# Rows of 272 values instead of 264 in two activation tiles of a two-block transformer kernel

## The chip, the cores and the metric

The kernel is one program on one core of a Trainium2 chip. The metric is the device time of one execution in microseconds (us). All arithmetic is float32; the large products are made from float32r operands, in which each factor is split into a high and a low part.

## The reference

256 tokens of width 1024 go through two blocks of two layers each. The first block is conditioned by vectors c and c_ctx: each layer has shifts, scales and gates from `silu(c) @ ada_w`. Its layers are a latent attention over 256 context and 256 own tokens, and a gated MLP with a token mixing; each is followed by a feed-forward layer of 4096:

```python
h = rmsnorm(x, g) * (1 + scale) + shift
x = x + g_m * mixer(h)
x = x + g_f * (square(relu(modulate(x) @ w1)) @ w2)
```

The second block has an even layer (gated linear attention in chunks of 64, and attention in a sliding window) and an odd layer (attention in blocks), each with one wide input projection of a normed x and one output projection. All matrices of weights are read from HBM once: some 190 MB.

## The kernel before, in words

The program writes out one stream of instructions for each engine and orders them with semaphores. Activations lie transposed: 128 features on the partitions, 256 tokens along the row, so a tensor of width 1024 is 8 k tiles of one row each.

The matrices come in chunks of 128 x 1024 values (512 KB) through a ring of 4 slots (`raw`). For each chunk ScalarE copies the float32r high part into `w_hi` (L1147), and VectorE writes `raw - w_hi` into `w_lo` (L1577). TensorE then makes every product of a weight tile and an activation row three times (`split_product`): L527 high by high, L528 weights' high part by the activation's low part, L529 weights' low part by the activation's high part. Each of the three is a weight load of 128 x 128 and a matmul that streams the row. Eight k tiles of three products make one group, whose sum stands in a PSUM bank; VectorE or ScalarE reads it out, and the other of two (or four) banks is filled meanwhile.

The activation rows are read from these tiles:

- `act_hi`, `act_lo`: 8 rows each, 264 values long (ACT_W). 256 are tokens; in the first block two more columns (256 and 257) hold the shift, so that one product makes both, and streams 258 columns (`act_and_shift`). Stages ffn0_up (32 groups), gm_u0 (8) and ffn1_up (32) read 258 columns; even_s, even_a, even_g, odd_g, odd_k and odd_q (37 groups) read 256 (`act`). Two token projections, even_av and odd_v, and the scores of the latent attention use parts of the rows as the weights.
- `hid_hi`, `hid_lo`: 32 rows of 256, read in ffn0_down and ffn1_down (32 groups of 24 products each).
- `s_hi`, `s_lo`: 16 rows of 256, read in gm_v (as weights), gm_u1 and gm_out; `om`, `oe`, `oo`: 8 rows of 256, read by the output projections of the attentions.

ffn0_down follows ffn0_up directly, and ffn1_down follows ffn1_up. In the up stages VectorE also scales each group (L1636), ScalarE applies relu and splits (L1380, L1383), GpSimd squares and subtracts (L2182, L2186), and VectorE takes the products for the next layers' shifts and scales (L1592), whose weights stream through a ring of their own. SyncE issues the loads in the order of use.

Two small tensors concern the change as well. `gqk` (128 x 1) is the product of two gains, written by VectorE at L1728, and the scale of the keys' eviction on ScalarE (L1289) and VectorE (L1760). `rms_gla` (8 x 128) holds the roots of the linear attention's mean squares: ScalarE writes it (L1167, called in L1513), VectorE inverts it (L2059), and TensorE spreads it over the partitions (L1063). `rstd` (128 x 512) holds the reciprocal roots of the token norms; behind the latent attention only columns 0 to 257 are in use.

SBUF is laid out in the order of the declarations, and tensors of different layers share addresses. In the even layer it is full to the last 128 bytes of a partition. By that order, `act_hi`, `act_lo`, `hid_hi`, `hid_lo`, `s_hi`, `s_lo`, `om` and `oo` begin at 64 bytes past a multiple of 256 in each partition, `w_hi`, `w_lo` and `oe` at 128.

Of the kernel before, what the change touches and what calls it, by code (L numbers as in the profile page):

```python
# [22 lines left out]
P = 128  # L23
D = 1024
KT = D // P
S = 256
CTX = 256
SC = S + CTX
H = 8
Q_LORA, KV_LORA, ROPE = 384, 256, 64  # L30
# [3 lines left out]
RING = 4  # L34
ADA_FIRST = 16
QK = 192
ACT_W = S + 8
TAU = 16.0
EPS = 1e-6
NEG = -1e30  # L40
# [106 lines left out]
def build_program(nc, vecs, consts, gm_rows, c_rows, rel_ext, x_in, ctx_in, ada, weights,  # L147
                  gm_ws, gla_w_up, out):
    fp32, fp32r = mybir.dt.float32, mybir.dt.float32r
    ALU, ACT, AX = mybir.AluOpType, mybir.ActivationFunctionType, mybir.AxisListType  # L150
# [10 lines left out]
    with hold:  # L161
        def sb(name, shape, dt=fp32, stack=hold):
            return stack.enter_context(nc.sbuf_tensor(name, shape, dt))

        def sem(name):
            return hold.enter_context(nc.semaphore(name))
# [12 lines left out]
        mod_in = sb("mod_in", [P, 2 * KT, 2])  # L179
        mods = sb("mods", [P, ADA_MODS, KT])  # L180
        gain = sb("gain", [P, 5, KT])
        eps_q = sb("eps_q", [P, 2])
        act_hi = sb("act_hi", [P, KT, ACT_W], fp32r)
        act_lo = sb("act_lo", [P, KT, ACT_W], fp32r)
        scaled = sb("scaled", [P, 2, S + 2])
# [4 lines left out]
        rstd = sb("rstd", [P, SC])  # L190
# [8 lines left out]
        with ExitStack() as mla:  # L199
            with ExitStack() as first:  # L200
                in_f32 = sb("mla_in", [P, 2, SC], fp32, first)
                in_hi = sb("mla_in_hi", [P, 2, SC], fp32r, first)
                in_lo = sb("mla_in_lo", [P, 2, SC], fp32r, first)
                ada_more = sb("ada_more", [P, 4, CW], fp32, first)
                unused = sb("products", [P, CW], fp32, first)
            kn_hi = sb("kn_hi", [P, H, SC], fp32r, mla)
            v_mla = sb("v_mla", [P, 4, H * P], fp32, mla)
            with ExitStack() as first:
                ctx = sb("ctx", [P, KT, CTX], fp32, first)
                sq_ctx = sb("sq_ctx", [P, KT, CTX], fp32, first)  # L210
                ckv = sb("ckv", [P, 2, SC], fp32, first)
                sq_lora = sb("sq_lora", [P, 3, SC], fp32, first)
                silu_ctx = sb("silu_ctx", [P, CW], fp32, first)
            kn_lo = sb("kn_lo", [P, H, SC], fp32r, mla)
            qr_hi = sb("qr_hi", [P, H // 2, S], fp32r, mla)
            qr_lo = sb("qr_lo", [P, H // 2, S], fp32r, mla)
            kpe_hi = sb("kpe_hi", [P, SC], fp32r, mla)
            kpe_lo = sb("kpe_lo", [P, SC], fp32r, mla)
            k_rstd_hi = sb("k_rstd_hi", [H, SC], fp32r, mla)
            k_rstd_lo = sb("k_rstd_lo", [H, SC], fp32r, mla)  # L220
            om_hi = sb("om_hi", [P, KT, S], fp32r, mla)
            om_lo = sb("om_lo", [P, KT, S], fp32r, mla)
            p_mla = sb("p_mla", [P, 2, SC], fp32, mla)
            pt_mla = sb("pt_mla", [P, 2, 4, S], fp32, mla)
            heads = sb("heads", [H, H], fp32r, mla)
            q_scale = sb("q_scale", [P, 2, 2, H], fp32, mla)
            gqk = sb("gqk", [P, 1], fp32, mla)
        late = hold.enter_context(ExitStack())
        bias = sb("bias", [P, 16, S], fp32, late)
        anti = sb("anti", [P, P], fp32, late)  # L230
# [16 lines left out]
        with ExitStack() as even:  # L247
            masks = sb("masks", [P, 2 * S + P], fp32, even)
            aq = sb("aq", [P, 2, S], fp32, even)
            ak = sb("ak", [P, 2, S], fp32, even)  # L250
            z_state = sb("z_state", [P, 4, S], fp32, even)
            z, zl = z_state[:, 0:2, :], z_state[:, 2:4, :]
            state = z_state[:, 0:3, :].rearrange("p n (t d) -> p n t d", t=2)
            cum = sb("cum", [P, 2, S], fp32, even)
            e_pos = sb("e_pos", [P, 2, S], fp32, even)
            e_neg = sb("e_neg", [P, 2, S], fp32, even)
            e_last = sb("e_last", [P, 2, S], fp32, even)
            down, w_up = e_last[0:16, 0, :], e_last[0:16, 1, :]
            qe = sb("qe", [P, 2, S], fp32, even)
            ke = sb("ke", [P, 2, S], fp32, even)  # L260
            kl = sb("kl", [P, 2, S], fp32, even)
            decay = sb("decay", [P, 2, 2, 4], fp32, even)
            kl_tok = sb("kl_tok", [P, 2, 2, P], fp32, even)
            av = sb("av", [P, 2, 512], fp32, even)
            att = sb("att", [P, H, P], fp32, even)
            bq = sb("bq", [P, 4, S], fp32, even)
            bk = sb("bk", [P, S], fp32, even)
            bv = sb("bv", [P, S], fp32, even)
            bv_tok = sb("bv_tok", [P, 2, P], fp32, even)
            gate = sb("gate", [P, H, S], fp32, even)  # L270
            rms_gla = sb("rms_gla", [H, P], fp32, even)
            o_gla = e_last
            logit = sb("logit", [P, 2, S], fp32, even)
            late_held = sb("late_held", [P, 2, S], fp32, even)
            held = [scaled[:, 0, 0:S], scaled[:, 1, 0:S], late_held[:, 0, :], late_held[:, 1, :]]
            prob = sb("prob", [P, 2, S], fp32, even)
            prob_t = sb("prob_t", [P, 4, 2, P], fp32, even)
            oe_hi = sb("oe_hi", [P, KT, S], fp32r, even)
            oe_lo = sb("oe_lo", [P, KT, S], fp32r, even)
# [12 lines left out]
        bank = [hold.enter_context(nc.psum_tensor(f"bank{i}", [P, 512], fp32)) for i in range(8)]  # L292
# [72 lines left out]
        cq_high, q_eps = sem("cq_high"), sem("q_eps")  # L365
# [1195 lines left out]
        def _(dve):  # L1561
# [18 lines left out]
            def modulate(a):  # L1580

                m, o = divmod(a, KT)
                dve.wait_ge(ada_in[a % RING], 16 * (a // RING + 1))
                dve.tensor_tensor_reduce(ada_raw[:, a % RING, :], ada_raw[:, a % RING, :], silu_row[:], 1.0,
                                         V("ada_b0", 2 * KT + a, 1), ALU.mult, ALU.add,
                                         mods[:, m, o:o + 1]).then_inc(ada_used, 1)
# [135 lines left out]
            modulate(1)  # L1722
            convert(11)
            dve.wait_ge(lora_sums, 1)
            dve.tensor_scalar(eps_q[:], bank[7][:, 0:2], EPS / Q_LORA, EPS * EPS, ALU.mult, ALU.add).then_inc(q_eps, 1)
            modulate(2)
            convert(12)
            dve.tensor_tensor(gqk[:], V("q_g_nope"), V("k_g_nope"), ALU.mult).then_inc(gqk_ready, 1)  # L1728
# [639 lines left out]
```

## Time and profile before

| | |
|---|---|
| median of 3 runs | 980.67 us (978.28 to 981.75) |
| the profiled execution | 979.0 us |
| its span, first to last instruction | 977.2 us |
| mean granted clock of TensorE | 0.977 |
| TensorE busy | 933.1 us, 95% |
| VectorE busy | 704.9 us, 72% |
| ScalarE busy | 537.5 us, 55% |
| GpSimd busy | 308.9 us, 32% |
| DMA | 195.60 MB, 200 GB/s |

The profile is of one execution, so its numbers are compared with 979.0 us. PE is the matmul side of TensorE, PEld its weight loads, which run beside the matmuls. A matmul's duration reaches over the start of the next ones, because they are pipelined: how fast they follow each other is read from their starts, or from how many there are in a window.

### The profile page before, as it was taken

Reading aid. Unit: us, or ns where it says so; the run is one execution under the profiler, and the core shown is the slowest. Engines: PE = TensorE matmul, PEld = TensorE weight load, DVE = VectorE, ACT = ScalarE, POOL = GpSimd, SP = SyncE. Lnnn points to the kernel's source line nnn. Section 1 sums busy time; section 2 is a strip of 40 time slices with the busy share of each in tenths; the row PEclk is TensorE's granted clock in tenths of the full one; section 3 lists DMA queues with packets and bytes.
Section 4 is the critical chain, followed back from the end, with each engine's and each line's share of the span. In section 5 each row is a group of like instructions: output and inputs, shape, how many; then the busy total and the mean of one; then the engine's idle time right before and its main releaser. Section 6 shows DMA issues by size and latency. Waiting matters only on the chain.

```text
span 977.2 us, 19548 instructions
## 1 busy us (share of the span) xinstructions
PE 933.1 (95%) x6882; PEld 861.5 (88%) x6882; DVE 704.9 (72%) x1132; ACT 537.5 (55%) x921; POOL 308.9 (32%) x272
## 2 busy tenths in 40 slices
PE   5988989999999999999979999999999999999996
PEld 5877556799999999988969999999999879899996
DVE  3997678678889788897886698555555873575764
ACT  3565655565666444655634666655444771674644
POOL 1952022227898011120051288640110000330012
PEclk9898999999999999999979999999999998999999
DMA  9856175167877988788615676555565332255421
GB/s 348 291 190 225 41 232 178 43 237 262 321 278 266 309 287 293 246 321 285 231 66 174 235 257 217 185 182 192 187 199 174 122 108 87 87 173 185 160 88 43
DMA packets 57052, 195.60 MB, mean 200 GB/s; under 512 B 6303, under 2 KB 9791, under 8 KB 56736
## 3 DMA queue, kind: packets, MB, share of 16 engines
q1 hardware_dynamic: 55312, 192.36, 58.0%
q0 software_dynamic: 1680, 2.44, 1.1%
q8 instruction: 37, 0.61, 0.3%
q14 instruction: 23, 0.19, 0.1%
HBM read 192.65 MB, written 1.07 MB: 198 GB/s over the span
## 4 chain that ended last, share of the span: by engine, by line
PE 84%; DVE 9%; ACT 3%; issue 3%; DMA 1%; POOL 0%; SPq 0%; DVEq 0%; ACTq 0%
PE bank L527 24%; PE bank L529 23%; PE bank L528 23%; DVE w_lo L1577 2%; PE bank L792 1%; PE bank L926 1%; PE bank L952 1%; PE bank L625 1%; ACT w_hi L1147 1%; PE bank L783 1%; DMA x<-x_in 1%; PE bank L825 1%; PE bank L634 1%; DVE ada_raw L1679 1%; PE bank L880 1%
## 5 line engine op out<-in xcount | busy, mean ns | idle before, releaser
L1577 DVE TENSOR_TENSOR w_lo<-raw,w_hi 128x1024 fp32r<-128x1024 f32 (+1 forms) x261 | 338.7, 1300 | 101.9 <-ACT w_hi L1147 99.4
L1147 ACT ACTIVATE w_hi<-raw 128x1024 fp32r<-128x1024 f32 (+1 forms) x261 | 272.4, 1045 | 166.6 <-PE bank L529 156.0
L527 PE MATMUL bank<-act_hi,w_hi 128*128 128x258 f32 (+1 forms) x872 | 251.1, 288 | 0.0
L529 PE MATMUL bank<-act_hi,w_lo 128*128 128x258 f32 (+1 forms) x872 | 247.5, 284 | 0.0
L528 PE MATMUL bank<-act_lo,w_hi 128*128 128x258 f32 (+1 forms) x872 | 246.1, 282 | 0.0
L527 PEld LDWEIGHTS bank<-act_hi,w_hi 128*128 128x128 f32 x872 | 166.5, 191 | 3.3 <-issue 2.8
L528 PEld LDWEIGHTS bank<-act_lo,w_hi 128*128 128x128 f32 x872 | 166.7, 191 | 1.0 <-issue 1.0
L529 PEld LDWEIGHTS bank<-act_hi,w_lo 128*128 128x128 f32 x872 | 165.6, 190 | 0.0
L528 PE MATMUL bank<-hid_lo,w_hi 128*128 128x256 f32 x512 | 141.4, 276 | 0.0
L527 PE MATMUL bank<-hid_hi,w_hi 128*128 128x256 f32 x512 | 141.4, 276 | 0.0
L529 PE MATMUL bank<-hid_hi,w_lo 128*128 128x256 f32 x512 | 141.4, 276 | 0.0
L528 PEld LDWEIGHTS bank<-hid_lo,w_hi 128*128 128x128 f32 x512 | 96.1, 188 | 0.0
L527 PEld LDWEIGHTS bank<-hid_hi,w_hi 128*128 128x128 f32 x512 | 96.1, 188 | 0.0
L529 PEld LDWEIGHTS bank<-hid_hi,w_lo 128*128 128x128 f32 x512 | 96.1, 188 | 0.0
L2182 POOL TENSOR_TENSOR tile_f<-relu 128x256 f32<-128x256 f32 x64 | 80.4, 1257 | 30.9 <-ACT relu L1380 30.9
L2186 POOL TENSOR_TENSOR hid_lo<-tile_f,hid_hi 128x256 f32 x64 | 75.1, 1173 | 18.0 <-POOL tile_f L2182 18.0
L2134 POOL TENSOR_TENSOR square_sum<-square_sum,sq 128x256 f32<-128x256 f32 x30 | 38.7, 1290 | 131.7 <-ACT sq L1179 131.7
L1592 DVE CUSTOM_DVE_ANT_0 ada_raw<-ada_raw,silu_row 128x1024 f32<-128x1024 f32 x56 | 75.8, 1354 | 2.3 <-DMA ada_raw<-ada 2.0
L2126 POOL TENSOR_TENSOR s_lo<-tile_f,s_hi 128x256 fp32r<-128x256 f32 x24 | 23.4, 993 | 98.2 <-ACT s_hi L1152 98.2
L527 PE MATMUL bank<-s_hi,w_hi 128*128 128x256 f32 x192 | 54.1, 282 | 0.0
L528 PE MATMUL bank<-s_lo,w_hi 128*128 128x256 f32 x192 | 53.7, 279 | 0.0
L529 PE MATMUL bank<-s_hi,w_lo 128*128 128x256 f32 x192 | 53.7, 279 | 0.0
(349 smaller groups left out, 1815.0 us busy)
## 6 DMA issues: line engine op xcount, KB each, us to landing
raw<-weights SPq DMA_DIRECT2D x247, 512.0 KB, 4.0
ada_raw<-ada SPq DMA_DIRECT2D x88, 512.0 KB, 4.9
raw<-weights SPq DMA_DIRECT2D x14, 384.0 KB, 4.6
ada_more<-ada SPq DMA_DIRECT2D x8, 512.0 KB, 6.6
bias<-bias_by_distance SPq DMA_DIRECT2D x1, 2048.0 KB, 9.3
x<-x_in SPq DMA_DIRECT2D x1, 1024.0 KB, 7.7
ctx<-ctx_in SPq DMA_DIRECT2D x1, 1024.0 KB, 9.7
out<-result SPq DMA_DIRECT2D x4, 256.0 KB, 2.7
```

Of the source, the lines that this page charges most:

```text
L527: pe.matmul(dst, w[0], a[0], start=start, stop=False)
L528: pe.matmul(dst, w[0], a[1], start=False, stop=False)
L529: return pe.matmul(dst, w[1], a[0], start=False, stop=stop)
L625: last = pe.matmul(bank[at_bank][:, 0:S], mean[:], source[:, k, :], start=k == 0, stop=k == KT - 1)
L634: last = pe.matmul(bank[6 + k % 2][:, 0:2], first_ada(2 * k)[:, j * P:(j + 1) * P], silu_c[:, j, :], start=j == 0, stop=j == KT - 1)
L1147: act.activation(w_hi[:, slot, 0:width_of(c)], raw[:, slot, 0:width_of(c)], ACT.Copy).then_inc(weight_hi, 1)
L1577: dve.tensor_tensor(w_lo[:, slot, 0:w], raw[:, slot, 0:w], w_hi[:, slot, 0:w].bitcast(fp32), ALU.subtract).then_inc(weight_lo, 1)
L1592: dve.tensor_tensor_reduce(ada_raw[:, q, :], ada_raw[:, q, :], silu_row[:], 1.0, 0.0, ALU.mult, ALU.add, ada_col[:, q:q + 1]).then_inc(ada ...
L2126: pool.tensor_tensor(lo, tile_f32[:, i % 4, :], hi.bitcast(fp32), ALU.subtract).then_inc(split_lo, 1)
L2134: pool.tensor_tensor(square_sum[:], sq[:, 0, :] if k == 1 else square_sum[:], sq[:, k, :], ALU.add).then_inc(square_sums, 1)
L2182: pool.tensor_tensor(tile_f32[:, i % 4, :], relu[:, g % 2, :], relu[:, g % 2, :], ALU.mult).then_inc(hid_squared, 1)
L2186: pool.tensor_tensor(hid_lo[:, ds(it * 8 + g, 1), :], tile_f32[:, i % 4:i % 4 + 1, :], hid_hi[:, ds(it * 8 + g, 1), :].bitcast(fp32), ALU. ...
```

## The change

ACT_W goes from S + 8 = 264 to S + 16 = 272 values, so a row of `act_hi` and `act_lo` takes 1088 bytes instead of 1056, and each tile 8704 instead of 8448. What is read and written of a row is as before. `gqk` becomes the third column of `eps_q`, and `rms_gla` a part of `rstd`: 8 partitions, columns 384 to 511.

```diff
-ACT_W = S + 8
+ACT_W = S + 16
...
-        eps_q = sb("eps_q", [P, 2])
+        eps_q = sb("eps_q", [P, 3])
...
-            gqk = sb("gqk", [P, 1], fp32, mla)
+            gqk = eps_q[:, 2:3]
...
-            rms_gla = sb("rms_gla", [H, P], fp32, even)
+            rms_gla = rstd[0:H, SC - P:SC]
...
-            dve.tensor_scalar(eps_q[:], bank[7][:, 0:2], EPS / Q_LORA, EPS * EPS, ALU.mult, ALU.add).then_inc(q_eps, 1)
+            dve.tensor_scalar(eps_q[:, 0:2], bank[7][:, 0:2], EPS / Q_LORA, EPS * EPS, ALU.mult, ALU.add).then_inc(q_eps, 1)
```

S is 256, SC 512, P 128 and H 8.

## Rows read from the trace of the kernel before

**Rows 1.** The page, part 1: busy us, share of the span, instructions.

```profile
PE 933.1 (95%) x6882; PEld 861.5 (88%) x6882; DVE 704.9 (72%) x1132; ACT 537.5 (55%) x921; POOL 308.9 (32%) x272
```

**Rows 2.** The page, part 4: the chain that ended last, by engine and line.

```profile
PE 84%; DVE 9%; ACT 3%; issue 3%; DMA 1%; POOL 0%; SPq 0%; DVEq 0%; ACTq 0%
PE bank L527 24%; PE bank L529 23%; PE bank L528 23%; DVE w_lo L1577 2%; PE bank L792 1%; PE bank L926 1%; PE bank L952 1%; PE bank L625 1%; ACT w_hi L1147 1%; PE bank L783 1%; DMA x<-x_in 1%; PE bank L825 1%; PE bank L634 1%; DVE ada_raw L1679 1%; PE bank L880 1%
```

**Rows 3.** Windows: from:to us, length, busy by engine (instructions), PE clock, DMA, GB/s.

```profile
230.00:300.00 70.00, 70.00 (x587) 70.00 (x586) 59.90 (x76) 44.98 (x73) 59.49 (x47) 1.00 0.85 299
310.00:390.00 80.00, 80.00 (x708) 80.00 (x708) 65.47 (x80) 37.23 (x47) 14.27 (x11) 1.00 0.86 291
470.00:486.00 16.00, 16.00 (x144) 16.00 (x143) 15.72 (x30) 10.62 (x17) 0.00 (x0) 1.00 0.61 209
510.00:550.00 40.00, 40.00 (x342) 40.00 (x341) 24.50 (x28) 19.37 (x27) 7.68 (x6) 1.00 0.53 171
854.00:866.00 12.00, 12.00 (x102) 12.00 (x102) 11.11 (x19) 9.62 (x17) 6.33 (x5) 1.00 0.72 226
876.00:896.00 20.00, 20.00 (x172) 20.00 (x171) 10.06 (x13) 9.51 (x14) 0.00 (x0) 1.00 0.47 150
575.00:640.00 65.00, 65.00 (x545) 65.00 (x545) 46.33 (x58) 42.48 (x68) 51.28 (x47) 1.00 0.65 211
655.00:730.00 75.00, 75.00 (x664) 75.00 (x663) 42.80 (x42) 33.67 (x42) 8.83 (x6) 1.00 0.60 190
```

**Rows 4.** Groups by line and shape, whole span: count, busy us, mean ns of one.

```profile
L527 PE MATMUL bank<-act_hi,w_hi 128*128 128x258 f32 x576 | 163.8, 284 | 0.0
L528 PE MATMUL bank<-act_lo,w_hi 128*128 128x258 f32 x576 | 161.9, 281 | 0.0
L528 PE MATMUL bank<-hid_lo,w_hi 128*128 128x256 f32 x512 | 141.4, 276 | 0.0
L528 PE MATMUL bank<-act_lo,w_hi 128*128 128x256 f32 x296 | 84.2, 284 | 0.0
```

**Rows 5.** Timeline, 304.1 to 307.0 us, L527 alone: start us, duration us.

```profile
304.11 0.29 PE L527 MATMUL bank<-act_hi,w_hi 128*128 128x258 f32 x1
...
304.48 0.29 PE L527 MATMUL bank<-act_hi,w_hi 128*128 128x258 f32 x1
...
304.84 0.28 PE L527 MATMUL bank<-act_hi,w_hi 128*128 128x258 f32 x1
...
305.20 0.28 PE L527 MATMUL bank<-act_hi,w_hi 128*128 128x258 f32 x1
...
305.56 0.28 PE L527 MATMUL bank<-act_hi,w_hi 128*128 128x258 f32 x1
...
305.92 0.28 PE L527 MATMUL bank<-act_hi,w_hi 128*128 128x258 f32 x1
...
306.28 0.28 PE L527 MATMUL bank<-act_hi,w_hi 128*128 128x258 f32 x1
...
306.63 0.28 PE L527 MATMUL bank<-act_hi,w_hi 128*128 128x258 f32 x1
...
306.99 0.29 PE L527 MATMUL bank<-hid_hi,w_hi 128*128 128x256 f32 x1
```

**Rows 6.** The tiles gqk and rms_gla: durations ns (min/median/max), first and last start.

```profile
L1728 DVE TENSOR_TENSOR gqk<-vec x1: 155/155/155, 74.9 to 74.9; 128x1 f32<-128x1 f32 x1
L1289 ACT ACTIVATE kn_hi<-bank,gqk x8: 681/682/683, 101.1 to 117.7; 128x512 fp32r<-128x512 f32 x8
L1760 DVE SCALAR_TENSOR_TENSOR kn_lo<-bank,gqk,kn_hi x8: 750/751/752, 101.9 to 118.4; 128x512 fp32r<-128x512 f32 x8
L1063 PE MATMUL bank<-rms_gla,const x16: 270/270/371, 842.3 to 844.1; 8*128 8x128 f32 x16
L2059 DVE RECIPROCAL rms_gla<-rms_gla x1: 940/940/940, 841.3 to 841.3; 8x128 f32<-8x128 f32 x1
```

## The prediction

> **What bounds the kernel now.** I read the engines' shares first: TensorE is busy 95% of the span, the weight loads that run beside it 88%, VectorE 72%, the others less [rows 1]. The chain that ended last says the same by another road: 84% of it lies on PE, and the three lines of the split product (L527, L528, L529) hold 70% of it [rows 2]. So the time is a count of fp32r products times the distance from one start to the next, wherever the products run gaplessly. The windows inside the dense stages give that distance: the window's length plus the 0.28 us that one product lasts, over the count of PE. In each of these windows PE is busy from end to end and its clock is the full 2.4 GHz. An edge can miscount one product, which is 0.2% in the long windows and 1% in the 12 us one.
>
> The answer is not one number [rows 3]:
> - rows of `act`, 258 columns (ffn0_up, ffn1_up): 70.28/587 = 119.7 ns and 65.28/545 = 119.8 ns
> - rows of `act`, 256 columns (odd_g): 20.28/172 = 117.9 ns
> - rows of `hid`, 256 columns (ffn0_down, ffn1_down): 80.28/708 = 113.4 ns and 75.28/664 = 113.4 ns
> - rows of `s`, 256 columns: 16.28/144 = 113.1 ns in gm_u1, but 40.28/342 = 117.8 ns in gm_out
> - rows of `oe`, 256 columns (even_out): 12.28/102 = 120.4 ns
>
> The mean durations of one product say the same: 276 ns from `hid`, 281 to 284 from `act` [rows 4]. The clock and the number of columns do not explain this: `hid`, `s` and `oe` have the same width, and two columns are 0.8 ns at 2.4 GHz. What differs is where a row begins. A row of `hid` or `s` is 1024 bytes, so all begin at one place modulo 256 (64, by the order and the sizes of the tensors). `oe` begins at 128 modulo 256, and the weights too. `act` rows are 1056 bytes apart, which is 4 x 256 + 32, so the eight k tiles step through 64, 96, 128, ... 32. But `s` shows that place is not all: the same rows cost 113.1 in one stage and 117.8 in another. There is some locking between the stream of moving rows and the stream of weight loads, into which a stage falls when it starts.
>
> **The change, part by part.**
>
> *gqk into a third column of eps_q.* It is written once (155 ns) and read as a scale by 8 ScalarE and 8 VectorE instructions [rows 6]. The instructions, their order and their waits stay; eps_q stays within the 32 bytes that it occupied. I take 0. The trace has no pair that differs in this alone; a bound either way is the whole write, 0.16 us.
>
> *rms_gla into rstd, partitions 0 to 7, columns 384 to 511.* The same root, reciprocal (940 ns) and 8 products (16 records of 270 ns) as before, in the same order [rows 6]. The row scaling of this layer reads columns 0 to 257 of rstd, so no new hazard and no wait. I take 0. Where both bounds matter, the largest thing in it is the reciprocal on the path, and 10% of that is 0.1 us each way. These two edits free 32 and 512 bytes, which is room for the longer rows (2 tiles x 8 rows x 32 bytes = 512). Everything behind the two tiles moves by 512 bytes or by nothing, so the place modulo 256 of all other operands stays.
>
> *Rows of 272.* No instruction is added, removed or widened: the products still read 258 or 256 columns. Rows are now 1088 bytes apart, 4 x 256 + 64. k tiles 0 to 7 begin at 64, 128, 192, 0, 64, 128, 192, 0, so all eight at multiples of 64, where now only the four even ones do. act_lo begins 256 bytes later, the same place modulo 256. What can change is the distance of 576 x 3 = 1728 products of 258 columns [rows 4] and of 296 x 3 = 888 of 256 columns. 144 more have an `act` row as the weights (16 of scores, 16 of each token projection on each of three lines); at 1% of the about 0.12 to 0.23 us that one lasts they hold 0.3 us either way, and I take 0.
>
> No row shows rows that are 64 apart modulo 256. The nearest ones:
> (a) The even rows of today's tiles already begin at multiples of 64. In the last group of ffn0_up, the starts of L527 are 0.37, 0.36, 0.36, 0.36, 0.36, 0.36, 0.35, 0.36 us apart for k = 0 to 7 [rows 5]. Even rows: 0.37 + 0.36 + 0.36 + 0.35 = 1.44; odd rows: 4 x 0.36 = 1.44. The aligned half is no cheaper. If all eight become like the even ones, the change is 0, with 0.02 us in 2.88 as reading error, 0.7% of 1728 x 0.12 = 207 us: 1.4 us either way.
> (b) The upper spacing of 64-aligned rows, 117.8 in gm_out, plus 0.8 for two columns: 1728 x (119.7 - 118.6) = 1.9 us gained, 888 x (117.9 - 117.8) = 0.1: together 2.0.
> (c) The lower spacing, 113.4 and 114.2: 1728 x 5.5 = 9.5 and 888 x 4.5 = 4.0, together 13.5 us gained. This is the lower end.
> (d) That of `oe`: taken at its round value of 120.0 within its 1%, 1728 x 1.1 + 888 x 2.1 = 3.8 us lost. This is the upper end for these products.
>
> I take the middle of (a) and (b), 1.0 us gained: (a) is measured on the very rows, the width and the weights concerned, and (b) and (c) come from tiles whose place stays fixed from k to k, which this change doesn't bring: the place still moves at each k, just in other steps. So I expect no lock on the fast spacing.
>
> The Trainium skill, page "TensorE: Matmul & The Clock Gate", section "Step-by-step: what each phase is for", says that streaming and weight loading have read ports of their own, so that loading doesn't take bandwidth from the running product; "SBUF — State Buffer", section "SBUF: two separate sides", puts a cost only on crossing 16-byte lines, and 1056 and 1088 are both multiples of 16. By these the change is worth exactly nothing. The spread of 113.1 to 120.4 ns at one width and clock disagrees with the first, so I don't let it decide.
>
> *What covers and what comes late.* If `act` products speed up, VectorE and GpSimd must keep up: in 230 to 300 us they are busy 59.90 and 59.49 of 70 us [rows 3], so 2.46 and 2.44 us of a group's 24 x 119.7 = 2.87. Even the fast case leaves 2.74. ScalarE has less, and 299 GB/s would have to become 313 in (c), which the trace doesn't show; if DMA stays at 299, ffn0_up (32 of the 72 groups) keeps its 9.5 x 32/72 = 4.2 us.
>
> **Sum.** The profiled execution took 979.0 us (span 977.2 and 1.8 around it). 979.0 - 1.0 = 978.0; its median of three runs is 980.67, 1.7 above, so 979.7. This kernel's runs differ by 0.3%, 2.9 us, so less than that counts as the same.
>
> **Rivals.**
> 1. *Fast lock.* Aligned rows let the `act` stages fall into the fast spacing wholly or in part. For it: both `hid` stages and gm_u1 have it, and all are 64-aligned. Against it: [rows 5] even rows gain nothing today. In full 13.5 us, 967.2; half of it (one width, or DMA holding ffn0_up) 974.
> 2. *The fast lock of ffn_down is lost (slower side).* ffn0_down and ffn1_down follow an `act` stage without a gap (the last start of [rows 5] is the first product of `hid`), and `s` shows that one tile can be in either state by how it is entered. If the new pattern of k hands over in another phase, 512 x 3 = 1536 products go from 113.4 to 117.8: 6.8 us. With the 1.0 gained: 980.67 + 5.8 = 986.5. It decides at the first product of ffn0_down, and holds for the stage. Against it: today both entries come out fast.
> 3. *Slow lock.* The `act` stages settle as `oe` does, case (d): 980.67 + 3.8 = 984.5.
> 4. *Nothing depends on the row's place*, as the ports' rule has it: 980.7.
>
> **Chances.** Forecast 0.37, fast lock 0.34, ffn_down lost 0.15, slow lock 0.08, nothing at all 0.06. Faster: 0.34. Same: 0.43 (forecast and 4). Slower: 0.23. The range reaches from 968, just inside the full fast lock, to 987, just over rival 2; I leave out some 0.08 below and 0.06 above. The forecast's own range is (b) to the upper reading error of (a): 978.7 to 982.1.
>
> **What would show it.** In windows of the same stages: 230 to 300 should count about 590 products (119 ns), 310 to 390 still 708, gm_out 342. A count of 612 or more in the first is rival 1, about 680 in 310 to 390 rival 2, 582 or fewer in the first rival 3. The L527 starts of one group should stay at 0.35 to 0.37 us, now repeating after four k instead of eight. PE counts, waits and the tail of the linear attention stay as they are; a longer stretch around 841 us would prove the two moved tiles wrong. The prediction is wrong if the distance in any dense stage moves by more than 1%.

## The result, and the profile after

The changed kernel takes 988.12 us in the median of 9 runs (982.62 to 990.08), the kernel before 980.92 (978.28 to 984.92, 9 runs). The ratio is 1.0055, 95% interval [1.0033, 1.0076]: slower, by some 5 to 7 us (the quotient of the two medians is 1.0073, inside the interval). The profiled execution took 988.59 us with a span of 986.6, so 9.4 us more span than before. In the runs below, one execution each of after_extra64 (1828.03 us), rows320 (1316.69 us) and the kernel before (1530.78 us) was slow as a whole; the medians hold them and the ratios don't.

The page of the changed kernel, part 1 and the first lines of part 4, against [rows 1, 2]:

```profile
PE 942.5 (96%) x6882; PEld 871.1 (88%) x6882; DVE 704.2 (71%) x1132; ACT 538.1 (55%) x921; POOL 308.8 (31%) x272
PE 82%; DVE 11%; issue 3%; ACT 3%; DMA 1%; POOL 0%; SPq 0%; DVEq 0%; ACTq 0%
PE bank L527 24%; PE bank L528 23%; PE bank L529 23%; DVE w_lo L1577 2%; PE bank L792 1%; DVE products L1679 1%; PE bank L926 1%; PE bank L625 1%; PE bank L952 1%; ACT w_hi L1147 1%; DVE ada_raw L1679 1%; PE bank L783 1%; DMA x<-x_in 1%; PE bank L825 1%; DVE ada_more L1679 1%
```

There are as many instructions as before. PE is busy 942.5 - 933.1 = 9.4 us longer, all of the difference; the others are as they were. The groups of part 5 say which products, against [rows 4]:

```profile
L528 PE MATMUL bank<-act_lo,w_hi 128*128 128x258 f32 (+1 forms) x872 | 246.4, 283 | 0.0
L528 PE MATMUL bank<-hid_lo,w_hi 128*128 128x256 f32 x512 | 143.9, 281 | 0.0
```

The `act` rows, the only ones whose step changed, are as slow as ever. The `hid` rows, which the change only moved by 512 bytes, went from 276 to 281 ns. The windows of the dense stages, columns as in [rows 3]:

```profile
230.00:300.00 70.00, 70.00 (x587) 70.00 (x586) 60.12 (x76) 45.17 (x73) 59.72 (x47) 1.00 0.86 301
310.00:390.00 80.00, 80.00 (x681) 80.00 (x680) 62.58 (x76) 36.21 (x46) 13.39 (x11) 1.00 0.82 283
470.00:486.00 16.00, 16.00 (x144) 16.00 (x143) 15.12 (x29) 10.21 (x16) 0.00 (x0) 1.00 0.65 214
575.00:640.00 65.00, 65.00 (x545) 65.00 (x544) 47.59 (x60) 42.30 (x69) 51.58 (x47) 1.00 0.66 217
655.00:730.00 75.00, 75.00 (x639) 75.00 (x639) 40.28 (x39) 31.97 (x39) 7.43 (x6) 1.00 0.58 188
```

In the `act` windows the counts are those of before, 587 and 545. In the two `hid` windows they are 681 for 708 and 639 for 664: 80.28/681 = 117.9 ns from product to product instead of 113.4. The `act` rows of 256 columns (odd_g) are as before too. The changed kernel has one product less than the kernel before [rows 3] in 20 us, which is within the edge error:

```profile
882.00:902.00 20.00, 20.00 (x171) 20.00 (x170) 10.38 (x15) 10.12 (x15) 0.00 (x0) 1.00 0.40 131
```

Whole stages, the changed kernel and then the kernel before:

```profile
217.90:307.00 89.10, 89.10 (x745) 89.09 (x745) 77.27 (x96) 58.18 (x92) 74.49 (x58) 1.00 0.83 288
307.10:397.40 90.30, 90.30 (x769) 90.30 (x768) 71.75 (x89) 40.54 (x51) 16.77 (x13) 1.00 0.81 281
651.10:741.40 90.30, 90.30 (x769) 90.30 (x769) 48.04 (x47) 39.71 (x48) 11.65 (x10) 1.00 0.57 186
851.00:875.50 24.50, 24.50 (x193) 24.50 (x193) 17.58 (x29) 15.78 (x30) 11.09 (x11) 0.93 0.46 147
881.50:922.30 40.80, 38.89 (x313) 38.47 (x312) 20.69 (x26) 19.18 (x26) 0.00 (x0) 0.96 0.48 157
```

```profile
217.80:306.90 89.10, 89.10 (x745) 89.10 (x745) 77.03 (x96) 58.20 (x92) 74.28 (x58) 1.00 0.81 287
307.00:393.90 86.90, 86.90 (x769) 86.90 (x768) 71.61 (x89) 40.17 (x51) 17.00 (x13) 1.00 0.86 293
647.70:734.70 87.00, 87.00 (x770) 87.00 (x769) 48.66 (x47) 39.34 (x48) 11.72 (x10) 1.00 0.61 192
844.30:867.40 23.10, 23.10 (x193) 23.03 (x193) 17.56 (x29) 15.79 (x30) 11.06 (x11) 1.00 0.50 158
873.40:912.80 39.40, 37.49 (x313) 37.07 (x312) 20.74 (x26) 19.21 (x26) 0.00 (x0) 1.00 0.51 167
```

ffn0_up takes 89.10 us in both. ffn0_down and ffn1_down take 3.4 and 3.3 us more: 6.7 of the 9.4. Another 1.4 + 1.4 us lie in even_out and odd_g, where the granted clock was 0.93 and 0.96 instead of 1.00 in this execution: for part of these stages it stood at the lower level (0.50 in 852 to 854 us). Is that the change or the execution? The other executions tell. Through the spans and mean clocks of 115 executions of the kernel before (from all rounds of the study) goes a straight line that falls by 8.3 us for each 0.01 of clock. The mean clock differs from run to run in both kernels alike: it is 0.970 to 0.979 in the nine executions of the changed kernel, 0.974 on average, and 0.973 on average in those 115. The two profiled executions differ by 0.004 (0.973 and 0.977), so about 3.3 us of the 9.4 go with the clock and not with the change. At equal clock the nine spans of the changed kernel lie 6.3 us above that line on average (4.9 to 8.7), which fits the 6.7 us of the two ffn_down stages. What is left is below 1 us in several places, of both signs; one of them is mla_out, where PE makes 108 products in 200 to 212 us instead of 104. The two moved small tensors cost nothing, as these lines of the changed kernel show beside [rows 6]:

```profile
L1289 ACT ACTIVATE kn_hi<-bank,eps_q x8: 680/682/684, 102.1 to 118.7; 128x512 fp32r<-128x512 f32 x8
L1063 PE MATMUL bank<-rstd,const x16: 270/270/371, 849.0 to 850.8; 8*128 8x128 f32 x16
```

### The profile page after: what moved, and what is told of

Same layout as the page of the kernel before. It is cut to its first block, busy times and chain, and to the rows that moved or that the text cites. A ratio compares the mean times of both kernels' runs of the same rounds, so it can differ in the third digit from the quotient of the medians.

```text
span 986.6 us, 19548 instructions
## 1 busy us (share of the span) xinstructions
PE 942.5 (96%) x6882; PEld 871.1 (88%) x6882; DVE 704.2 (71%) x1132; ACT 538.1 (55%) x921; POOL 308.8 (31%) x272
## 3 DMA queue, kind: packets, MB, share of 16 engines
q0 software_dynamic: 1680, 2.44, 1.1%
## 4 chain that ended last, share of the span: by engine, by line
PE 82%; DVE 11%; issue 3%; ACT 3%; DMA 1%; POOL 0%; SPq 0%; DVEq 0%; ACTq 0%
PE bank L527 24%; PE bank L528 23%; PE bank L529 23%; DVE w_lo L1577 2%; PE bank L792 1%; DVE products L1679 1%; PE bank L926 1%; PE bank L625 1%; PE bank L952 1%; ACT w_hi L1147 1%; DVE ada_raw L1679 1%; PE bank L783 1%; DMA x<-x_in 1%; PE bank L825 1%; DVE ada_more L1679 1%
## 5 line engine op out<-in xcount | busy, mean ns | idle before, releaser
L527 PE MATMUL bank<-act_hi,w_hi 128*128 128x258 f32 (+1 forms) x872 | 249.6, 286 | 0.0
L527 PEld LDWEIGHTS bank<-act_hi,w_hi 128*128 128x128 f32 x872 | 165.6, 190 | 3.3 <-issue 2.8
L527 PE MATMUL bank<-hid_hi,w_hi 128*128 128x256 f32 x512 | 143.9, 281 | 0.0
L528 PE MATMUL bank<-hid_lo,w_hi 128*128 128x256 f32 x512 | 143.9, 281 | 0.0
L529 PE MATMUL bank<-hid_hi,w_lo 128*128 128x256 f32 x512 | 143.9, 281 | 0.0
L527 PEld LDWEIGHTS bank<-hid_hi,w_hi 128*128 128x128 f32 x512 | 97.2, 190 | 0.0
L527 PE MATMUL bank<-s_hi,w_hi 128*128 128x256 f32 x192 | 54.1, 282 | 0.0
```

The source lines that it names most:

```text
L527: pe.matmul(dst, w[0], a[0], start=start, stop=False)
L528: pe.matmul(dst, w[0], a[1], start=False, stop=False)
L529: return pe.matmul(dst, w[1], a[0], start=False, stop=stop)
```

## The experiments

Each kernel ran beside the kernel before. In the table, the three counts are of PE in 230 to 300, 310 to 390 and 655 to 730 us (ffn0_up, ffn0_down, ffn1_down); 708 and 664 are the fast spacing, 681 and 639 the slow one. The counts are of one profiled execution each. rows320_width256 leaves out the two shift columns, so its output lacks the shifts.

| kernel | median us | ratio to before [95%] | ffn0_up | ffn0_down | ffn1_down |
|---|---|---|---|---|---|
| before | | | 587 | 708 | 664 |
| changed | 988.12 | 1.0055 [1.0033, 1.0076] | 587 | 681 | 639 |
| rows264_rest512 | 980.82 | 1.0011 [0.9987, 1.0035] | 587 | 709 | 664 |
| edits_only | 981.49 | 1.0005 [0.998, 1.0031] | 587 | 709 | 664 |
| rows272_hid1024 | 987.3 | 1.0068 [1.0048, 1.0089] | 587 | 682 | 639 |
| rows264_lo256 | 980.32 | 0.9985 [0.9962, 1.0007] | 587 | 708 | 664 |
| before_extra128 | 980.85 | 1.0012 [0.9985, 1.0038] | 587 | 709 | 664 |
| before_extra64 | 988.85 | 1.0086 [1.0058, 1.0113] | 587 | 681 | 639 |
| after_extra128 | 980.63 | 0.9999 [0.9976, 1.0021] | 587 | 708 | 664 |
| after_extra64 | 987.07 | 1.0028 [0.9999, 1.0057] | 587 | 682 | 639 |
| after_kick_inside | 983.07 | 1.0015 [0.9988, 1.0041] | 587 | 699 | 657 |
| rows320 | 984.06 | 1.0024 [1.0003, 1.0046] | 582 | 682 | 664 |
| rows320_width256 | 978.3 | 1.0001 [0.9966, 1.0036] | 608 | 698 | 664 |
| rows260 | 982.95 | 1.0012 [0.9984, 1.004] | 582 | 708 | 665 |
| rows268 | 986.1 | 1.006 [1.0029, 1.0091] | 584 | 681 | 639 |
| before_kicks | 982.12 | 1.0006 [0.9983, 1.003] | 588 | 709 | 664 |

Do the profiled counts speak for the other executions of a kernel? Against the same line of span and clock, the kernels with both ffn_down stages slow (changed, rows272_hid1024, before_extra64, rows268) lie 5.8 to 7.4 us above it on average, those with both fast (rows264_rest512, edits_only, rows264_lo256, before_extra128, after_extra128, before_kicks, rows260) 0.8 below to 1.2 above, and rows320, with one slow stage, 3.3 above. So in most of these kernels the state of the ffn_down stages holds from execution to execution.

### Which part of the change: rows264_rest512, edits_only, rows272_hid1024, rows264_lo256

```diff
 # all against the changed kernel; rows264_rest512:
-ACT_W = S + 16
+ACT_W = S + 8
         act_lo = sb("act_lo", [P, KT, ACT_W], fp32r)
+        gap = sb("gap", [P, P])
 # edits_only: the first line alone
 # rows272_hid1024:
+            gap = sb("gap", [P, P], fp32, ffn)
             hid_hi = sb("hid_hi", [P, FFN // P, S], fp32r, ffn)
 # rows264_lo256: ACT_W = S + 8, and
+        gap = sb("gap", [P, P // 2])
         act_lo = sb("act_lo", [P, KT, ACT_W], fp32r)
+        gap_2 = sb("gap_2", [P, P // 2])
```

> The changed kernel with rows of 264 again and 512 unused bytes behind act_lo, so that every tensor behind it stays where the change put it. Two theories for the 3.4 us that each ffn_down stage lost (113.4 to 117.8 ns from product to product). H, handover: the stream of act rows enters the stage in another phase because its rows are 1088 bytes apart. P, place: the hid tiles themselves moved by 512 bytes. H expects the fast state back: some 708 products in 80 us of ffn0_down, 981 us. P expects 681 in 80 us and 988 us.

> The changed kernel with rows of 264: only gqk and rms_gla stand in their new places, and nothing in front of the even layer's last tiles moves. Both H and P expect the time of before, 981 us, and 708 products in 80 us of ffn0_down. If these two edits cost anything themselves, this is over 982.5.

> The changed kernel with 512 unused bytes in front of hid_hi: rows of 272, but hid_hi and hid_lo 1024 bytes behind where before has them, so at its place modulo 1024. H expects no help: 681 products in 80 us, 988 us. P expects 708 and 981 us.

> The changed kernel with rows of 264, but act_lo 256 bytes farther behind act_hi, where the change put it, and everything behind them also where the change put it. The change did two things to the act rows: the step from row to row, and the distance between high and low rows (8448 to 8704 bytes, 256 to 0 modulo 512). H1: the step decides the state of ffn_down; expects 708 products in 80 us of ffn0_down and 981 us. H2: the distance decides; expects 681 and 988 us.

ffn0_down of the first and of the third:

```profile
310.00:390.00 80.00, 80.00 (x709) 80.00 (x708) 65.47 (x80) 37.04 (x47) 13.93 (x10) 1.00 0.84 291
```

```profile
310.00:390.00 80.00, 80.00 (x682) 80.00 (x681) 62.56 (x76) 36.19 (x46) 13.35 (x11) 1.00 0.80 283
```

With rows of 264 the stage is fast wherever `hid` lies; with rows of 272 it is slow in both of its places. P falls. The two small edits are worth nothing that can be measured. rows264_lo256 is fast, so it is the step from row to row and not the distance from high to low rows: H1. With everything else in place, the `hid` products are slowed by a change in the rows that were read ahead of them.

### Is it the handover: before_extra128, before_extra64, after_extra128, after_extra64, after_kick_inside

```diff
 # *_extra64 and *_extra128 (n = 64 or 128), ahead of the loop of ffn_down:
+                pe.matmul(bank[7][:, 0:n], act_hi[:, KT - 1, 0:P], act_hi[:, KT - 1, 0:n], start=True, stop=True)
                 with pe.Fori(0, 4) as it:
                     for i in range(8):
 # after_kick_inside, n = 128, inside:
+                        if i == 1:
+                            pe.matmul(...)
                         pe.wait_ge(weight_lo, at(chunk0[down_] + i + 1, it, 8))
```

> The kernel before with one extra product of 128 columns into an unused bank right ahead of each ffn_down stage (two in the program); no address changes. H expects that the entry can decide the state: either stage may fall to 117.8 ns (681 products in 80 us, 3.4 us each, up to 988 us), and if it stays fast, the cost is 0.2 us in all. P expects that nothing but 0.2 us changes: 981 us and 708 products.

> The kernel before with one extra product of 64 columns into an unused bank right ahead of each ffn_down stage. H, the handover decides by phase: what 64 columns did not mend in the changed kernel they may break here; if a stage falls to 117.8 ns, 681 products in 80 us of ffn0_down and 984 to 988 us, with no address changed. If the rows of 264 give the fast state whatever comes between, 708 and 981 us.

> The changed kernel with one extra product of 64 columns into an unused bank right ahead of each ffn_down stage; no address changes. H, the handover decides: a different entry may bring the fast state back in one or both stages: 981 to 985 us, 708 products in 80 us of ffn0_down. If the state were a property of the stage with these rows whatever comes ahead, 681 and 988 us.

> As after_extra64 with 128 columns: under H the state is a matter of phase, so 64 and 128 columns may differ; fast again: 981 to 985 us, else 988 us.

> The changed kernel with an extra product of 128 columns not ahead of the ffn_down stages but inside: after the first of every eight chunks, so four in each stage. If the two spacings are states that each hold until something shifts the phase (H), the first eight products of a stage are at 117.8 ns and the rest at 113.4 from the first extra product on: 708 in 80 us of ffn0_down, 981 us. If an extra product helps only where it stands between act and hid rows, 681 and 988 us.

The kernel before with one extra product of 64 columns at each entry, no address changed:

```profile
310.00:390.00 80.00, 80.00 (x681) 80.00 (x681) 62.54 (x76) 36.09 (x46) 13.37 (x11) 1.00 0.81 282
655.00:730.00 75.00, 75.00 (x639) 75.00 (x638) 39.95 (x39) 32.33 (x39) 7.69 (x6) 1.00 0.57 188
```

The changed kernel with one of 128 columns:

```profile
310.00:390.00 80.00, 80.00 (x708) 80.00 (x707) 65.61 (x81) 37.66 (x48) 14.82 (x11) 1.00 0.83 290
655.00:730.00 75.00, 75.00 (x664) 75.00 (x663) 43.35 (x42) 33.25 (x42) 8.83 (x6) 1.00 0.60 193
```

Two extra products of some 0.1 us cost the kernel before 0.86% [0.58, 1.13], and two of double the width give the changed kernel all that it lost. before_extra64 and before_extra128 have the same instructions at the same places and differ only in the columns of that product. So the spacing belongs neither to the tiles nor to the step alone: it is a state into which the stage falls when it starts, and which it keeps unless something shifts it. That 128 columns leave before fast and 64 leave the changed kernel slow in its profile fits, but neither was foretold by more than "may". The trace does not resolve what differs: from the extra product to the second product of `hid` it shows 0.22 us with 64 columns (307.12 to 307.34) and with 128 (307.36 to 307.58). The other runs of after_extra64 spread from 979 to 989 us, and at equal clock they lie 2.6 to 7.9 us above the line of the kernel before, so in some of them one of the two stages may have been fast. That isn't shown: only the one execution was profiled.

after_kick_inside shows a state broken in mid-stage (the extra products stand at 313.92 and 336.64 us, and about 22 us apart after that):

```profile
315.00:336.00 21.00, 21.00 (x181) 21.00 (x180) 17.17 (x21) 9.51 (x13) 4.99 (x4) 1.00 0.87 309
338.00:358.00 20.00, 20.00 (x179) 20.00 (x178) 15.60 (x20) 7.99 (x10) 1.86 (x2) 1.00 0.81 283
360.00:380.00 20.00, 20.00 (x179) 20.00 (x178) 15.91 (x21) 8.12 (x10) 1.85 (x2) 1.00 0.86 286
```

21.28/181 = 117.6 ns after the first extra product, 20.28/179 = 113.3 after the second and from then on. In ffn1_down too it was the second (675.6 us), not the first (652.9 us):

```profile
654.00:675.00 21.00, 21.00 (x181) 21.00 (x179) 10.26 (x11) 8.19 (x11) 0.04 (x1) 1.00 0.59 191
677.00:697.00 20.00, 20.00 (x179) 20.00 (x178) 10.79 (x11) 8.05 (x10) 1.80 (x2) 1.00 0.62 200
```

I had expected the first to do it, and 981 us instead of 983.07. One product of 128 columns turns slow to fast only at times, and it left fast as it was in each of the cases seen.

### Place and width: rows320, rows320_width256, rows260, rows268

```diff
 # rows320 (rows260, rows268: S + 4, S + 12 and 128 unused bytes before and behind act_lo)
-ACT_W = S + 16
+ACT_W = S + 64
...
-            k_rstd_hi = sb("k_rstd_hi", [H, SC], fp32r, mla)
-            k_rstd_lo = sb("k_rstd_lo", [H, SC], fp32r, mla)
+            k_rstd_hi, k_rstd_lo = (t[0:H, :, S:S + 64] for t in (act_hi, act_lo))
...
-            logit = sb("logit", [P, 2, S], fp32, even)
-            late_held = sb("late_held", [P, 2, S], fp32, even)
+            logit, late_held = (ada_raw[:, i, 0:2 * S].rearrange("p (a b) -> p a b", a=2) for i in range(2))
...
 # rows320_width256: that, and
-                return act_hi[:, k, 0:S + 2], act_lo[:, k, 0:S + 2]
+                return act_hi[:, k, 0:S], act_lo[:, k, 0:S]
...
```

> The changed kernel with rows of 320 values, 1280 bytes, 5 x 256: all act rows begin at the same place modulo 256 (64), as those of hid and s do. Room for them: the two parts of the keys' inverse root stand in the spare columns of the rows, and logit and late_held of the even layer in ada_raw, which is unused by then. Theory F: a stage can lock into the fast spacing only if its rows keep their place from k to k, so the act stages have 119.7 ns because they step. It expects 114.2 to 118.6 ns in ffn0_up (592 to 615 products in 70 us instead of 587), up to 9.5 us less for 258 columns and 4 us less for 256: 967 to 980 us. Rival W: 119.7 ns belongs to the width of 258 columns; then 587 products stay, and only the stages of 256 columns gain or nothing: 977 to 988 us, depending on the state of ffn_down.

> The kernel with rows of 320 with the two shift columns left out of the products of the first block (they stream 256 columns instead of 258), so its output lacks the shifts; nothing else is changed. It tells the width from the place. Theory F (a stage whose rows keep their place has the states of 113.4 and 117.8 ns) expects ffn0_up at 592 to 617 products in 70 us, 967 to 978 us. If the row tiles themselves are slow, 120 ns and 980 us.

> The changed kernel with rows of 260 values, 1040 bytes, 4 x 256 + 16, and all tiles behind them where the kernel before has them. If only the step of 1088 loses the entry to ffn_down: 708 products in 80 us, 981 us. If any step but 1056 does: 681 and 988 us. For the act stages: 119.7 ns at 1056 and 1088 alike, so 119.7 here (587 products in 70 us) if the step doesn't matter while the rows move; nearer to the 120.8 of rows that keep their place if a small step acts like none.

> As rows260 with 268 values, 1072 bytes, 4 x 256 + 48, and all tiles behind them where the change put them. Only 1088 loses the entry: 708 and 981 us; any step but 1056: 681 and 988 us. act stages at 587 products in 70 us.

ffn0_up, ffn0_down and ffn1_down of rows320, then ffn0_up and ffn1_up of rows320_width256:

```profile
230.00:300.00 70.00, 70.00 (x582) 70.00 (x581) 60.40 (x76) 45.29 (x73) 59.65 (x47) 1.00 0.85 300
310.00:390.00 80.00, 80.00 (x682) 80.00 (x681) 61.93 (x76) 35.65 (x45) 12.69 (x10) 1.00 0.82 283
655.00:730.00 75.00, 75.00 (x664) 75.00 (x663) 41.31 (x41) 33.14 (x41) 8.11 (x6) 1.00 0.59 193
```

```profile
230.00:300.00 70.00, 69.53 (x608) 69.11 (x608) 59.31 (x75) 44.70 (x70) 58.52 (x47) 1.00 0.85 300
575.00:640.00 65.00, 65.00 (x576) 65.00 (x575) 50.65 (x61) 45.92 (x73) 57.88 (x49) 1.00 0.68 223
```

Theory F is half right. Rows that keep their place reach the fast spacing when 256 columns stream (65.28/576 = 113.3 ns in ffn1_up), but with 258 columns they are the slowest of all, 70.28/582 = 120.8 ns. The two shift columns cost 7.5 ns there, and not the 0.8 that their two cycles are. So rows320 loses in the first block. In odd_g, in the second, it has 14.28/122 = 117.0 ns against 117.9 before, which is within the edge error of 0.8%. rows320 also has one ffn_down stage slow and the other fast, with the same tiles and the same entry code.

The time of rows320_width256 did not follow: 978.3 us and a ratio of 1.0001, where 967 to 978 was expected. ffn1_up gains in full, but ffn0_up does not, and the count of 698 in ffn0_down is low for another reason than the spacing. The chain that ended last in 240 to 300 us, and two windows of ffn0_down:

```profile
by line: POOL tile_f L2181 45.5%; POOL hid_lo L2185 27.5%; issue 22.3%; POOLq L2185 1.7%; POOLq L2184 1.0%; ACT relu L1379 0.9%; POOLq L2180 0.9%; DVE scaled L1635 0.7%; POOLq L2177 0.4%; POOLq L2183 0.2%; ACTq L1378 0.0%
309.00:312.00 3.00, 3.00 (x16) 3.00 (x15) 2.72 (x4) 2.27 (x4) 2.73 (x4) 0.50 0.79 294
320.00:390.00 70.00, 70.00 (x620) 70.00 (x619) 54.97 (x69) 32.19 (x41) 8.84 (x6) 1.00 0.84 292
```

At the faster spacing a group of ffn0_up takes PE 24 x 113.3 ns = 2.72 us, but GpSimd's two instructions for it repeat every 2.90 us (`tile_f` starts at 297.70 and, two groups later, at 303.50). So PE gets ahead of GpSimd, and at the entry of ffn0_down it waits 2.78 us for VectorE's scaling (L1635), which is behind in the same chain. After that wait the granted clock falls to 0.50 for some 3 us, and from 320 us on the stage is fast, 70.28/620 = 113.4 ns. This stage was entered with a gap. DMA isn't what holds ffn0_up: 300 GB/s, the mean of the window, isn't its limit, since 240 to 260 us alone have 363, and the chain lies on GpSimd and not on transfers. In ffn1_up GpSimd keeps up. Its second instruction takes mostly 0.75 us there (629 to 640 us), where in ffn0_up it alternates between 0.74 and 1.42.

The rows of ffn0_down of rows260 and of rows268:

```profile
310.00:390.00 80.00, 80.00 (x708) 80.00 (x708) 64.19 (x77) 36.43 (x47) 14.37 (x11) 1.00 0.81 285
```

```profile
310.00:390.00 80.00, 80.00 (x681) 80.00 (x680) 61.82 (x76) 35.49 (x45) 12.78 (x10) 1.00 0.78 283
```

A step of 1040 keeps the fast entry, 1072 loses it (982.95 and 986.1 us). Both simple readings fall, "only 1088" and "any step but 1056". Steps of 1056 and 1088 give 119.7 ns in the `act` stages, 1072 gives 70.28/584 = 120.3 and 1040 gives 120.8.

### A try at a version that beats both: before_kicks

```diff
+                    for i in project("gm_out", 16, ...):
+                        if i < 2:
+                            pe.matmul(bank[7][:, 0:128], act_hi[:, KT - 1, 0:P], act_hi[:, KT - 1, 0:128], start=True, stop=True)
...
 # and the same in mla_out
```

> The kernel before with extra products of 128 columns inside mla_out (after its first and second group) and gm_out (after the first and second chunk of each eight), which were both at 117.8 ns in its profile and at 113.4 ns in others. H: two such products bring a stage to 113.4 ns and leave it there: mla_out some 0.6 us and gm_out some 1.5 us shorter where they would have been slow, 0.7 us spent on six products; 979 to 981 us, best case the fastest correct kernel so far. If these stages are slow for another reason, 981.5 us.

In its profile mla_out (108 products in 200 to 212 us, before 104) and gm_out are fast. But mla_out has 108 in the changed kernel as well, and gm_out is fast in edits_only, both without an extra product. The first window below is of the kernel before, the second of edits_only, the third of before_kicks:

```profile
515.00:525.00 10.00, 10.00 (x87) 10.00 (x86) 6.66 (x7) 5.35 (x8) 1.47 (x1) 1.00 0.49 155
```

```profile
515.00:525.00 10.00, 10.00 (x90) 10.00 (x89) 6.93 (x8) 5.16 (x8) 1.47 (x1) 1.00 0.55 175
```

```profile
515.00:525.00 10.00, 10.00 (x90) 10.00 (x90) 6.87 (x8) 4.51 (x8) 1.47 (x1) 1.00 0.47 160
```

The ratio of 1.0006 [0.9983, 1.003] does not tell it from before. So it isn't shown that the extra products brought either stage to the fast spacing. No kernel of this study is shown to beat the kernel before.

## Why the prediction was wrong

*What bounds the kernel* was read rightly: the time is a count of products times their spacing, and the loss that belongs to the change, 6.7 us, came through the spacing.

*gqk and rms_gla at 0*: right (edits_only, 1.0005).

*The act rows* (1.0 us gained, between "like the even rows" and "like gm_out"): ffn0_up is 89.10 us in both profiles, so (a) was the right row and (b) the wrong one to average it with. That is 1.0 us of error. The starts within a group were to stay at 0.35 to 0.37 us, now repeating after four k. The order of a group of the changed kernel is, again L527 alone, for k = 0 to 3, at 304.22, 304.59, 304.94 and 305.30 us:

```profile
304.22 0.28 PE L527 MATMUL bank<-act_hi,w_hi 128*128 128x258 f32 x1
...
304.59 0.28 PE L527 MATMUL bank<-act_hi,w_hi 128*128 128x258 f32 x1
...
304.94 0.28 PE L527 MATMUL bank<-act_hi,w_hi 128*128 128x258 f32 x1
...
305.30 0.28 PE L527 MATMUL bank<-act_hi,w_hi 128*128 128x258 f32 x1
...
305.66 0.28 PE L527 MATMUL bank<-act_hi,w_hi 128*128 128x258 f32 x1
...
307.09 0.28 PE L527 MATMUL bank<-hid_hi,w_hi 128*128 128x256 f32 x1
```

They do stay there: the first four take 1.44 us and the last four 1.43. Whether they repeat can't be told. Starts are read to 0.01 us, and k = 0 with 0.37 and k = 4 with 0.36 differ by no more than that. By the same token [rows 5] could not show that the odd rows cost what the even ones do to better than the 0.7% that the prediction allowed for. Rival 3's price was low as well: (d) took 120.0 ns where [rows 3] gives 120.4, with which it is 4.8 us and not 3.8.

*What covers*: VectorE and GpSimd were to keep up even in the fast case, 2.44 us of GpSimd in a group of 2.74. That counted busy time alone. Between GpSimd's two instructions of a group lie 0.27 us of waiting, and in the trace of before they already repeat every 2.90 us near the end of ffn0_up (`tile_f` at 296.22 and, two groups later, at 302.02). rows320_width256 shows it: at a group of 2.72 us ffn0_up hangs on GpSimd. The gain of (c) in ffn0_up was priced too high, and DMA was the wrong reason for doubting it.

*The step that failed* is the one that was left implicit in the sum: that the `hid` stages keep 113.4 ns because "the place modulo 256 of all other operands stays". The prediction knew from gm_u1 and gm_out [rows 3] that place alone doesn't fix the spacing, and made the loss of the fast entry rival 2, at 15%, for the weak reason that both entries come out fast today. That both do is one observation made twice, since both follow the same `act` pattern, and the change altered just this pattern. Rival 2 is what happened, with its mechanism (before_extra64, after_extra128), at its place and at its price: 6.8 us forecast, 3.4 + 3.3 measured; its 986.5 us stands against 988.12 measured. Without the 1.0 gained it would have been 987.5. The range ended at 987.0, cut just above a rival whose own size had an error. So the mechanism was named, but as a side case: the forecast itself put the term of ffn_down at nothing.

*The fast lock of act* (0.34) did not happen, and rows320 speaks against it for 258 columns: even rows at a fixed place have 120.8 ns there. Both pieces that spoke for it, `hid` and gm_u1, had 256 columns, and the prediction took the width as worth 0.8 ns from the clock. That was the estimate to distrust.

*The ports' rule* of the Trainium skill ("TensorE: Matmul & The Clock Gate", "Step-by-step: what each phase is for") would have given no change, against the 6.7 us measured: taken as a rule for the time it failed. Whether the two ports themselves are independent, as the page says, no run here shows; nor does any run show that the weight loads have a part in the two spacings, as the prediction supposed.

Open stays what sets the phase at an entry. Steps of 1040 and 1056 entered fast, 1072 and 1088 slow, 1280 with 258 columns once each; an extra product of 64 columns broke a fast entry, one of 128 mended a slow one. Open too is why mla_out and gm_out are fast in some profiles and slow in others, among kernels that differ in nothing near them.

## What to carry to other kernels

Where products run gaplessly, read the spacing of each stage from its count before touching a layout, and compare stages that stream alike: a stage that is 4% slower than its twin may be in another state, and a state can be lost by a change of what runs ahead of it. A stage whose data and code aren't touched is not safe if it is entered without a gap from one that is; price it as part of the change. And test a layout by the counts in all dense stages, not by the one that it was meant for. Before putting a difference between two profiled executions down to a change, compare their mean clocks: here 0.004 of clock went with 3.3 us.

## What the runs showed of the hardware

- fp32r products of 256 columns at full clock follow each other in 113.4 or 117.9 ns with the same addresses (ffn0_down of before and of before_extra64, 708 and 681 products in 80 us). The ffn_down stages kept their spacing to the end where nothing stood between their products. In after_kick_inside the second of four extra products changed it from 117.6 to 113.3 ns.
- Two more columns can cost more than the 0.8 ns of their cycles: 7.3 ns in ffn1_up at a step of 1280 bytes (65.28/541 = 120.7 ns in rows320, 65.28/576 = 113.3 in rows320_width256). Against rows of 256 columns that are themselves at 117.9 ns (odd_g) it is 1.9 ns, at a step of 1056. 258 columns never came below 119.7 ns, at steps of 1040, 1056, 1072, 1088 and 1280 bytes.
- The rows of `oe`, which begin at the same place modulo 256 as the weights, had 120.4 ns in the kernel before [rows 3]. That the place is the cause was not tested.
- Making all rows begin at a multiple of 64 bytes (the changed kernel) gained nothing for either width: 587 products in 70 us with 258 columns in both kernels, and 171 in 20 us against 172 with 256 columns.
